# Key and value projections of a hybrid decoder step as three one-pass products of split operands, 512 columns a job

## What is computed

```python
def kv_rows(x, g_kv, w_kv):
    h = rms_norm(x, g_kv)
    kv = (h @ w_kv).reshape(x.shape[0], x.shape[1], N_BRANCH, 2, KV_HEADS, HEAD_DIM)   # w_kv: 1024 x 1536
    return kv[:, :, 0], kv[:, :, 1], kv[:, :, 2]

x = x + rms_norm(y @ a_w_out, a_norm_post)           # end of layer one
cmp, slc, win = kv_rows(x, kv_norm, w_kv)            # keys and values of the three branches
u = rms_norm(x, b_norm_pre) @ b_w_in                 # queries, gates and z of layer two
```

## Time and profile before

| | |
|---|---|
| time, three runs | 991.15, 993.01, 1070.59 us (median 993.01) |
| the profiled execution | 990.91 us |
| its span, first to last instruction | 989.1 us |
| PE busy | 920.6 us, 93% |
| DVE, ACT, POOL busy | 503.2, 421.7, 301.0 us |

### The profile page before, as it was taken

The page is one execution under the profiler, slowest core; times in us unless marked ns, Lnnn a source line. Parts: engine busy times, 40 slices in busy tenths (PEclk is TensorE's granted clock), DMA queues, the critical chain, the costliest instruction groups (busy, mean ns, idle before and its releaser), DMA issues. The chain is left out here.

```text
span 989.1 us, 16539 instructions
## 1 busy us (share of the span) xinstructions
PE 920.6 (93%) x6238; PEld 774.8 (78%) x6238; DVE 503.2 (51%) x1131; ACT 421.7 (43%) x872; POOL 301.0 (30%) x311
## 2 busy tenths in 40 slices
PE   2799999998999999998998899999999999799995
PEld 2699999944479878887998878878988888587663
DVE  2477999965843450212011255555555564635663
ACT  4356677523412411311223256555656555513321
POOL 0269888771460000003000033343332432500000
PEclk9999999999999999999999899999999999999998
DMA  8345443157446051135543222222222100932621
GB/s 213 85 107 170 118 111 77 49 167 256 153 121 215 38 173 53 33 96 127 135 85 85 45 43 65 44 65 66 43 55 52 46 2 2 243 132 66 179 91 32
DMA packets 156069, 97.40 MB, mean 98 GB/s; under 512 B 97156, under 2 KB 144932, under 8 KB 155911
## 3 DMA queue, kind: packets, MB, share of 16 engines
q1 hardware_dynamic: 141134, 77.07, 29.3%
q0 software_dynamic: 4896, 10.32, 3.1%
q10 hardware_dynamic: 9961, 8.97, 2.8%
HBM read 87.48 MB, written 18.85 MB: 108 GB/s over the span
## 5 line engine op out<-in xcount | busy, mean ns | idle before, releaser
L725 ACT ACTIVATE arena<-psum 128x256 f32<-128x256 f32 (+10 forms) x221 | 89.2, 441 | 217.5 <-PE psum L1623 58.6
L1623 PE MATMUL psum<-arena 128*128 128x256 f32 (+2 forms) x832 | 170.5, 367 | 1.2 <-issue 1.2
L1623 PEld LDWEIGHTS psum<-arena 128*128 128x128 f32 (+1 forms) x832 | 146.5, 190 | 22.6 <-issue 2.3
L1244 DVE SCALAR_TENSOR_TENSOR psum<-arena,psum 128x512 f32<-128x512 f32 x168 | 127.0, 756 | 6.0
L704 POOL TENSOR_SCALAR arena<-arena,kept 128x512 f32<-128x512 f32 (+3 forms) x128 | 82.7, 661 | 141.5 <-DVE kept L1490 141.5
L1943 PE MATMUL psum<-u_hi,tile_hi 128*128 128x288 f32 x352 | 113.1, 321 | 8.4 <-ACT arena L725 7.7
L1642 PE MATMUL psum<-h_hi,tile_hi 128*128 128x288 f32 x384 | 115.2, 300 | 4.1 <-DVE tile_lo L1216 4.1
L1643 PE MATMUL psum<-h_lo,tile_hi 128*128 128x288 f32 x384 | 114.6, 299 | 0.0
L1644 PE MATMUL psum<-h_hi,tile_lo 128*128 128x288 f32 x384 | 114.2, 297 | 0.0
L1944 PE MATMUL psum<-u_lo,tile_hi 128*128 128x288 f32 x352 | 104.3, 296 | 0.0
L1945 PE MATMUL psum<-u_hi,tile_lo 128*128 128x288 f32 x352 | 103.8, 295 | 0.0
(11 more groups left out here) (256 smaller groups left out, 1655.8 us busy)
## 6 DMA issues: line engine op xcount, KB each, us to landing
tile_whole<-in_b_w_in SPq DMA_DIRECT2D x64, 256.0 KB
tile_whole<-in_a_w_in SPq DMA_DIRECT2D x24, 512.0 KB
arena<-in_cmp_w SPq DMA_DIRECT2D x3, 2048.0 KB, 9.7
arena<-in_w_kv SPq DMA_DIRECT2D x6, 1024.0 KB, 12.2
bias_copies<-bias_line POOLq DMA_DIRECT2D x4, 1280.0 KB, 24.1
arena<-in_x_prompt SPq DMA_DIRECT2D x8, 512.0 KB, 10.2
arena<-in_a_w_out SPq DMA_DIRECT2D x4, 1024.0 KB, 16.8
arena<-bias_copies SPq DMA_DIRECT2D x16, 256.0 KB, 3.7
```

The lines of the kernel that those rows point to most:

```text
L725: return nc.scalar.activation(out, in_, ACT.Copy, scale=scale)
L1244: V.scalar_tensor_tensor(out=acc_p, in0=glu_p[:, m, w:w + SEQ], scalar=tap, in1=acc_p, op0=ALU.mult, op1=ALU.add).then_inc(S["conv_step"], 1)
L1623: ins = pe.matmul(out, l, r, start=(k == 0), stop=(k == len(pairs) - 1))
```

## The change

The 30 jobs become 15, one for each branch and block: 24 fp32r products of 512 columns each (keys and values of a branch together in one PSUM bank), for the eight slices hi by hi, rows hi by weights lo, rows lo by weights hi. The 64 sample rows take a job of their own like the others and no longer run side by side. The rows are split block by block and the six weight chunks one by one: ACT writes the hi parts (`kv_rows_hi`, `kv_weight_hi`), DVE the lo parts in place of the whole ones (`kv_rows_lo`, `kv_weight_lo`). The first two chunks are split inside the loop that ends layer one, the others later. `k_stage` moves, the weight slots are taken in another order, and `u_hi` is made only after job 9, since it lies where branch 1's hi weights are. The first three query tiles' `split_hi` now stand after all key and value jobs.

```diff
+            def kv_rows_hi(t):
+                act.wait_ge(S["hu_ready"], 2 * (t + 1))
+                act.wait_ge(S["o_mm"], t + 1)
+                here = slice(t * P, t * P + rows(t))
+                copy(kvh_hi[:, :, here], kvh_whole[:, :, here]).then_inc(S["hh_ready"], 1)
+            def kv_weight_hi(c):
+                act.wait_ge(place[C_KV + c][2], arrived[C_KV + c])
+                if c >= 4:
+                    act.wait_ge(S["kv_mm"], 5)
+                copy(kvw_hi(c // 2)[:, c % 2], kvw_whole[:, (4, 5, 0, 1, 2, 3)[c]]).then_inc(S["hi_ready"], 1)
@@ ACT, end of each block t of layer one
+                if t >= 2:
+                    kv_rows_hi(t - 2)
+                if t in (2, 3):
+                    kv_weight_hi(t - 2)
+            kv_rows_hi(TT - 2)
+            kv_rows_hi(TT - 1)
@@ ACT, the jobs
-            for n in range(30):
-                if n == 24:
-                    split_hi(0)
-                    split_hi(1)
+            for n in range(3 * TT):
+                if n in (1, 2):
+                    kv_weight_hi(n + 1)
+                if n in (6, 7):
+                    kv_weight_hi(n - 2)
+                if n == 2 * TT:
+                    act.wait_ge(S["kv_mm"], 2 * TT)
+                    for m in range(KD):
+                        copy(u_hi[:, m], uT[:, m]).then_inc(S["uh_ready"], 1)
...
-            split_hi(2)
+            act.wait_ge(S["kv_mm"], 3 * TT)
+            for j in range(3):
+                split_hi(j)
@@ DVE, end of block t, behind xn_b
+                    if t >= 3:
+                        kv_rows_lo(t - 3)
+                    if t in (3, 4):
+                        kv_weight_lo(t - 3)
+            for t in range(2, TT):
+                kv_rows_lo(t)
+            for c in range(2, 6):
+                kv_weight_lo(c)
@@ PE
-            for n in range(30):
-                c, t = kv_jobs[n]
-                await_chunk(C_KV + c)
+            def three(out, w, x, first, last):
+                pe.matmul(out, w[0], x[0], start=first, stop=False)
+                pe.matmul(out, w[0], x[1], start=False, stop=False)
+                return pe.matmul(out, w[1], x[0], start=False, stop=last)
+            for n in range(3 * TT):
+                br, t = n // TT, n % TT
+                pe.wait_ge(S["lo_ready"], 1 + 2 * br + 2)
                 if n == 2:
                     turn_b(TT - 1)
...
+                if n < 5:
+                    pe.wait_ge(S["hl_ready"], TT + (2, 2, 4, 4, 5)[n])
...
+                for k in range(KD):
+                    ins = three(pb(kv_bank(n), 2, CH)[0:r], [h[:, k, tokens] for h in (kvh_hi, kvh_lo)],
+                                [w[:, :, k] for w in (kvw_hi(br), kvw_lo(br))], k == 0, k == KD - 1)
+                ins.then_inc(S["kv_mm"], 1)
-                if n == 23:
+                if n == 12:
                     kt_transposes(0)
```

More of the change, by code:

```diff
@@ L279, in kv_bank, with kvw_hi, kvw_lo @@
             return (2, 3, 0, 1, 4, 5)[n % 6]
+        def kvw_hi(br):
+            return kvw_near if br == 1 else kvw_far
+        def kvw_lo(br):
+            first = (4, 0, 2)[br]
+            return kvw_rest[:, first:first + 2]
         def rows_slot(n):
@@ L352, in build @@
             else:
-                i = (4, 5, 3, 0, 1, 2)[c - C_KV] if C_KV <= c < C_Q else c % RING if c < C_KV else c - C_OB
+                i = (4, 5, 0, 1, 2, 3)[c - C_KV] if C_KV <= c < C_Q else c % RING if c < C_KV else c - C_OB
                 place[c] = (2 * D * i, 2 * D, w_in[i])
-        kv_jobs = {kv_at(c, t): (c, t) for c in range(6) for t in range(TT)}
         waited = {}
@@ L963, in _ @@
-                copy(dst, src).then_inc(S["kv_ready"], 1)
-                if n % 10 < 9:
+                act.wait_ge(S["kv_mm"], n + 1)
+                for kind in range(2):
+                    here = slice(0, rows(t))
+                    src = pb(kv_bank(n), 2, CH)[here, kind]
+                    if br == 0 and t < 4:
+                        dst = cmp_rows[:, t // 2, kind, :, HD * (t % 2):HD * (t % 2) + HD]
+                        src = src.rearrange("p (k d) -> p k d", d=HD)
+                    elif br == 0:
+                        dst = cmp_rows_s[here, kind * CH:(kind + 1) * CH]
+                    else:
+                        dst = (v_sb if kind else k_stage)[here, br - 1, t]
+                    copy(dst, src).then_inc(S["kv_ready"], 1)
@@ L1848, in _ @@
                 if n < 2:
-                    pe.wait_ge(S["hu_ready"], 2 * (n + 1))
                     pe.wait_ge(S["o_scaled"], 4)
                 elif n < 6:
-                    pe.wait_ge(S["hu_ready"], 2 * TT if n >= 4 else 2 * (n + 1))
                     pe.wait_ge(S["o_scaled"], TT)
+                    pe.wait_ge(S["hu_ready"], 2 * TT if n >= 4 else 8)
                 else:
-                    pe.wait_ge(S["kv_ready"], n - 5)
-                if t < 4:
-                    if c < 2:
-                        lhs = hT[:, :, (t // 2) * 256 + t % 2:(t // 2) * 256 + 256:2]
-                    else:
-                        lhs = hT[:, :, t * P:(t + 1) * P]
-                    product(pb(kv_bank(n), CH), ((lhs[:, k], chunk_sb(C_KV + c)[:, k]) for k in range(KD))).then_inc(S["kv_mm"], 1)
-                elif c % 2:
-                    for k in range(KD):
-                        for kind in range(2):
-                            ins = pe.matmul(pb(kv_bank(n - 1 + kind), CH, p0=kind * NS, p1=kind * NS + NS), hT[:, k, SEQ:NT],
-                                            chunk_sb(C_KV + c - 1 + kind)[:, k], start=(k == 0), stop=(k == KD - 1))
-                            if k == KD - 1:
-                                ins.then_inc(S["kv_mm"], 1)
-                if n == 23:
+                    pe.wait_ge(S["kv_ready"], 2 * (n - 5))
+                if n < 5:
+                    pe.wait_ge(S["hl_ready"], TT + (2, 2, 4, 4, 5)[n])
+                r = rows(t)
+                tokens = slice((t // 2) * 256 + t % 2, (t // 2) * 256 + 256, 2) if br == 0 and t < 4 else slice(t * P, t * P + r)
+                for k in range(KD):
[3 more added lines that the diff above has]
+                if n == 12:
                     kt_transposes(0)
```

63 lines of the change are left out of this document (34 added, 29 removed).

## The result

The changed kernel takes 1005.89 us (median of four runs, 1003.49 to 1007.74), the kernel before 992.52 in the same comparison: a ratio of 1.0127 with a 95% interval of 1.0100 to 1.0154. It is slower by 1.3%, and the interval does not contain 1. It lies 7.4 us above the forecast, inside the range of 993 to 1007. One of the four executions of the kernel before was a slow one (1070.59 us), and the ratio leaves it out. The same kernel taken once more gave 1006.21 and 1.0139 (1.0114 to 1.0165), so the loss is some 13 us. The profiled execution took 1005.07 us with a span of 1003.2, at a mean granted clock of 0.976; before it was 990.91, 989.1 and 0.992. What follows splits the 14.1 us between these two spans.

What follows compares the result with a forecast made beforehand. PE was taken to bound the stage, its shift reaching the program's end one for one. -16.3 + 10.6 + 3.9 + 4.75 + 3.4 = +6.4 us on 990.9, or 997.3, set at 998.5 after the close runs; range 993 to 1007.

Steps and rivals of the forecast that it cites:

- The products: Key and value jobs on PE: 360 fp32r products at 0.217 us replace 94.4 us of work, a gain of 16.3 us.
- The start: Before job 0: PE idles until DVE's subtractions for block 1 and weight chunk 1 end, job 0 at 370.4, +10.6 us.
- The stop at job 2: After job 1: subtractions for blocks 2 and 3 stand behind DVE's writing of block 4, so job 2 waits, +3.9 us.
- The clock in the stage: Half clock on PE after the idle times before jobs 0 and 2: +3.4 us for both, ends 0 and 5.
- The end of the stage: Last window-key transposes: DVE's copies queue behind the first two query tiles' subtractions, so PE waits longer, +4.75 us.
- What is hidden: Later chunk splits, `u_hi` and `u_lo` lie beside jobs and cost nothing; a lost cover would cost 2 to 5 us.
- signs of being wrong: Product starts over 0.22 apart, waits in jobs 3 to 14, query products before 477 or after 485, long half clock.
- A: Key and value jobs: fp32r stream slower, 0.236 us a product in proportion to 288 columns; 1005.4 us, chance 0.25.
- B: Key and value stage: PE stays at half clock for a good part; 1012 us and more, chance 0.03.
- C: Stage's start and end: waits shorter because DVE reaches subtractions sooner and query tiles' halves are ready; 983.4 us, chance 0.10.
- D: Key and value jobs: fp32r spacing independent of width, 0.133 us at 512 columns too; 968 us, chance 0.02.

Runs made afterwards that it cites:

- experiment on widths: Changed kernel with jobs 6, 7, 8 and 10 cut into fp32r products of 64 to 448 columns, all else the same; 1010.6 us.
- plain: Changed kernel with its 15 jobs of 512 columns in plain float32, no key or value halves made; 1009.10 us, ratio 1.0176.
- experiment with dummy products: Changed kernel with 11 unread float32 products keeping PE busy in its wait ahead of job 0; 1004.17 us, ratio 1.0115.
- halves: x_all with two products of 256 columns for each one of 512, keys first, then values; 985.05 us, ratio 0.9918.
- x_all: Changed kernel with DVE's subtractions for block 1, weight chunk 1 and blocks 2 and 3 earlier, first two query tiles' later; 982.71 us, ratio 0.9910.
- x_start: Changed kernel with DVE's subtractions for block 1 and weight chunk 1 moved ahead of the last block's chain; 994.34 us, ratio 1.0017.

## Why the prediction was right or wrong

- **The products: the step that failed.** The sum took 360 x 0.217, on the reasoning that 0.133 at 288 columns was a limit per instruction. The mean spacing over the stage is 0.2315, 360 x 0.0145 = 5.2 us more, and the gain is 11.1 instead of 16.3. The mechanism was right, the size off. The experiment on widths shows why: the 13 ns by which 288 columns exceed their stream are an addition that wide products pay too, 16 to 21 ns at 512 columns. The forecast had exactly this reading as 0.226 and as 0.236 and set it aside, because at half clock and at 48 weight columns nothing seemed added. Half clock did not bear on it: there 512 columns also go at (390.19 - 388.49)/4 = 0.425, the bare stream of 1.2 GHz, while at full clock they pay 18 ns. The Trainium skill, "TensorE: Matmul & The Clock Gate", section "Back-to-back issue gap", would give 0.216 for 512 columns by its formula, columns over 2.4 plus 2.5 ns. This case's runs have 0.216 for a pass of the plain float32 form (6.92/32 in plain) and 0.231 for fp32r, so the formula holds here for the one and not for the other.
- **The start:** forecast +10.6 and job 0 at 370.4, behind L1355; measured 370.65 behind L1355. 0.5 of the measured shift is from before the change (PE reached the stage that much later).
- **The stop at job 2:** forecast 4.5 after `turn_b(4)`, measured 387.92 - 383.48 = 4.44, behind L1351.
- **The clock in the stage:** forecast 3.4 for both waits, measured 1.7 + 1.6 = 3.3. The experiment with dummy products confirms the first by 1.5.
- **The end of the stage:** forecast +4.75, measured +4.55, behind L1428. The wait itself was the forecast one; but the thin stretch also holds a clock loss, which I called paid. Removing the wait removed that too, so it was worth 6.2, not 4.7.
- **What is hidden:** right. No job from 3 to 14 waited. DVE's and ACT's work beside the products cost nothing.
- **What was not in the sum:** 14.1 - 11.4 = 2.7 us behind the query products. The forecast took it that the shift of the query products goes into the end one for one, and put everything behind them at nothing. Of these 1.7 are the half clock near 930 (3.4 us of work) and 0.9 the longer one near the end; the remaining differences are of some tenths either way. No instruction there was changed. Of the nine variants only halves, which has no long wait left, has the one near 930. So it follows from none of the three waits. What decides it stays open.

Together: 6.4 forecast + 5.2 (spacing) + 0.25 (start) - 0.1 - 0.2 + 2.7 = 14.25, against 14.1 measured. Two of the forecast's own signs of being wrong came true: fp32r starts more than 0.22 apart, and query products that begin after 485 (485.97). It also said that only about 20 us can be told from no change; the interval of 1.0100 to 1.0154 tells 13 us from nothing.

Of the rivals, A came nearest: its 0.236 gave 1005.4, the measured time, but partly by luck, since with 0.2315 it would be 1003.7 and the rest is the clock behind the stage. I gave it 0.25 against the forecast's 0.60, though the one row of its type at full clock spoke for it. B fell: the clock was back about 3.3 us of work after each stop. C named the right remedy (DVE reaching the subtractions sooner, the tail's wait gone) for a kernel that didn't have it; x_all, which has it, is at 982.71, where C said 983.4, though by other sums. D fell with 0.231.

## What to carry to other kernels

An operation that feeds a matmul stage must stand in its engine's order where its data are ready, not where the loop that makes them ends: here three such places cost 22 us, more than the faster products gave (11), and moving them cost nothing. When a type's rate is known at one width only, take the proportion as the middle and not as the far end; an excess over the bare stream is an addition until a second width shows otherwise. A wait of some us ahead of dense work is to be priced with the half clock behind it, and a thin stretch that gets longer pays too. The gain of one removed wait is not to be read from the time alone: the half clock at the other waits moves with it.

## What the runs showed of the hardware

- Runs of fp32r products went at 0.108 us from start to start with 64 columns and at 0.109 with 128; from 256 columns on a product took the columns at 2.4 GHz and 12 to 21 ns more. A plain float32 pass of 512 columns took 0.216, so the same columns stream 7% slower as fp32r at full clock; at half clock the addition vanished (0.425 for 512 columns).
- The spacing differed by 2% between branches (0.229 to 0.231 against 0.234) with the same shapes, and did so with the operand in one piece (0.227 to 0.235). In the third branch it was 0.229 also while DVE, ACT and the transfers were idle. The cause is open.
- Removing one clock drop made a later one longer: with PE kept busy ahead of job 0 the stop at job 2, unchanged in itself, was followed by 6.8 us at half clock instead of 3.4, and the thin stretch by 13.7 instead of 6.8. With the wait ahead of job 0 ordered away (x_start) the thin stretch also had 13.7 us at half clock.
